# Encoder trunk on one core: the gate and up products of the large experts computed with the weights as the stationary operand

## What is computed

```
def swiglu(x, w_gate, w_up, w_down):
    return (jax.nn.silu(x @ w_gate) * (x @ w_up)) @ w_down

def moe_swiglu(x, w_router, w_gate, w_up, w_down):
    logits = (x @ w_router).astype(jnp.float32)
    top_v, top_i = lax.top_k(logits, TOP_K)
    gates = jax.nn.softmax(top_v, axis=-1)
    combine = jnp.sum(jax.nn.one_hot(top_i, N_EXPERTS, dtype=jnp.float32) * gates[..., None], axis=-2)
    out = jnp.zeros_like(x)
    for e in range(N_EXPERTS):
        out = out + combine[..., e:e + 1].astype(x.dtype) * swiglu(x, w_gate[e], w_up[e], w_down[e])
    return out
```

## Time and profile before

| | us |
|---|---|
| median of 3 runs | 1141.0 (1136.15 to 1141.62) |
| the profiled execution | 1139.2 |
| its span, from the first to the last instruction | 1137.3 |
| PE busy in the span | 1104.1 |
| PEld busy | 811.8 |
| DVE busy | 642.9 |
| ACT busy | 467.5 |

### The profile page before, as it was taken

One profiled execution on the slowest core, in us unless ns is written; L12 is line 12 of the kernel. 1 busy time (PEld: TensorE's weight loads), 2 busy tenths in 40 slices (PEclk: granted clock), 3 DMA queues, 4 the chain that ended last, 5 costly groups with the idle time before them and its releaser, 6 DMA issues.

```text
span 1137.3 us, 14580 instructions
## 1 busy us (share of the span) xinstructions
PE 1104.1 (97%) x5825; PEld 811.8 (71%) x5825; DVE 642.9 (57%) x745; ACT 467.5 (41%) x598; POOL 44.0 (4%) x45
## 2 busy tenths in 40 slices
PE   7999999999999999999999999999999999999996
PEld 6777878888877788776666666666666666666664
DVE  3887675445467886755655534554653465555235
ACT  4656444444335565143444423333343343443220
POOL 3000020000013000000000000000000000000001
PEclk9999999999999999989999999999999999999999
DMA  9943355555547600079999999899999989999972
GB/s 294 347 151 111 112 181 190 185 185 185 184 150 210 225 1 1 1 269 386 359 368 353 359 350 380 291 395 386 336 389 363 379 290 382 372 353 377 353 277 78
DMA packets 126815, 300.08 MB, mean 264 GB/s; under 512 B 4971, under 2 KB 7161, under 8 KB 126737
## 3 DMA queue, kind: packets, MB, share of 16 engines
q1 hardware_dynamic: 124336, 291.52, 71.1%
q0 software_dynamic: 2112, 6.87, 2.2%
q10 hardware_dynamic: 288, 0.63, 0.1%
HBM read 297.88 MB, written 1.12 MB: 263 GB/s over the span
## 4 chain that ended last, share of the span: by engine, by line
PE 88%; DMA 5%; DVE 2%; ACT 2%; issue 2%; POOL 0%; SPq 0%; POOLq 0%; DVEq 0%; ACTq 0%
PE bank L1595 23%; PE bank L1596 22%; PE bank L1657 12%; PE bank L2040 6%; PE bank L1685 6%; PE bank L2050 4%; PE bank L1768 3%; PE bank L1877 2%; DMA raw<-in_w_in 2%; PE bank L1862 1%; PE bank L1794 1%; PE bank L2018 1%; PE bank L1954 1%; DMA raw<-in_moe_w_gate 1%; PE bank L1600 1%
## 5 line engine op out<-in xcount | busy, mean ns | idle before, releaser
L1435 DVE TENSOR_TENSOR w_lo<-raw,w_hi 128x2048 fp32r<-128x2048 f32 x83 | 190.3, 2293 | 271.7 <-ACT w_hi L908 271.6
L1595 PE MATMUL bank<-w_hi,xT_hi 128*128 128x512 f32 (+1 forms) x832 | 331.7, 400 | 6.0 <-DVE xT_lo L1054 2.1
L1596 PE MATMUL bank<-w_hi,xT_lo 128*128 128x512 f32 (+1 forms) x832 | 321.7, 388 | 0.0
L908 ACT ACTIVATE w_hi<-raw 128x2048 fp32r<-128x2048 f32 x83 | 158.7, 1912 | 239.2 <-PE bank L1657 133.0
L1595 PEld LDWEIGHTS bank<-w_hi,xT_hi 128*128 128x128 f32 x832 | 157.1, 189 | 72.4 <-issue 28.5
L1031 DVE TENSOR_TENSOR w_lo<-raw,w_hi 128x2048 fp32r<-128x2048 f32 x62 | 141.9, 2291 | 104.8 <-ACT w_hi L727 104.4
L1596 PEld LDWEIGHTS bank<-w_hi,xT_lo 128*128 128x128 f32 x832 | 157.4, 189 | 28.8
L1657 PE MATMUL bank<-w_lo,xT_hi 128*128 128x512 f32 (+1 forms) x640 | 167.4, 384 | 0.0
L727 ACT ACTIVATE w_hi<-raw 128x2048 fp32r<-128x2048 f32 x64 | 122.6, 1918 | 99.5 <-PE bank L1657 45.9
L1657 PEld LDWEIGHTS bank<-w_lo,xT_hi 128*128 128x128 f32 x640 | 118.3, 188 | 24.2
L1595 PE MATMUL bank<-w_hi,hT_hi 128*128 128x512 f32 x312 | 124.7, 400 | 2.3 <-issue 2.3
(11 more groups left out here) (209 smaller groups left out, 1016.0 us busy)
## 6 DMA issues: line engine op xcount, KB each, us to landing
raw<-in_moe_w_up SPq DMA_DIRECT2D x70, 1024.0 KB, 8.8
raw<-in_moe_w_down SPq DMA_DIRECT2D x70, 1024.0 KB, 8.0
raw<-in_moe_w_gate SPq DMA_DIRECT2D x69, 1024.0 KB, 8.5
raw<-in_w_in SPq DMA_DIRECT2D x23, 1024.0 KB, 8.5
raw<-in_ffn_w_gate SPq DMA_DIRECT2D x11, 1024.0 KB, 5.1
raw<-in_ffn_w_up SPq DMA_DIRECT2D x11, 1024.0 KB, 5.1
raw<-in_ffn_w_down SPq DMA_DIRECT2D x11, 1024.0 KB, 5.0
raw<-in_w_out SPq DMA_DIRECT2D x8, 1024.0 KB, 5.9
```

Of the source, the lines that this page charges most:

```text
L908: nc.scalar.activation(w_hi[:, m % NH, :], raw[:, n % NR, :], ACT.Copy).then_inc(hi_done, 1)
L1435: nc.vector.tensor_tensor(w_lo[:, m % NH, :], raw[:, (BASE_MOE + load[at[o]]) % NR, :], w_hi[:, m % NH, :].bitcast(F32), ALU.subtract).the ...
L1595: nc.tensor.matmul(o, hi, wh, start=start, stop=False)
L1596: nc.tensor.matmul(o, lo, wh, start=False, stop=False)
```

## The change

`hidden_tiles` takes the place of `column_units` for the gate and up units of large experts. A 128 x 128 tile of the weights is stationary; one matmul moves the high and the low part of all 256 tokens past it side by side (512 columns; the new tile `xT` holds both parts next to each other), and one of 256 columns moves the high part past the low part of the weights. A unit is then 16 matmuls of 512 columns and 16 of 256. A chunk's gate or up result comes out as four tiles (`j`), hidden columns in the partitions, each in one bank: 256 columns of high and 256 of low part, which remain to be added. The tiles take five banks (0 to 4) in turn, `tile_bank`. DVE adds the two halves of each tile by a `tensor_reduce` (`read_tiles`) into `hidT`, the same memory as `hid`, or, for up, into a new tile `upT`; ACT applies silu to `hidT` in place and copies it to `hT_hi`; DVE multiplies and makes `hT_lo`. The transposes and their semaphore `e_psum` are gone; `tile_done` (PE to DVE) and `tile_read` (DVE to PE and ACT) are new.

```
-            def large_gate(c, eb):
-                if c > 0:
-                    act.wait_ge(e_psum, eb + 2 * c)
-                for tt in range(NT):
-                    ins = nc.scalar.activation(hid[:, tt, :], bank[:, tt, :], ACT.Silu)
-                ins.then_inc(silu_done, 1)
+            def large_gate(c, cb, tiles):
+                act.wait_ge(tile_read, tiles + (tile_at("gate", c, 3) + 1))
+                nc.scalar.activation(hidT, hidT, ACT.Silu).then_inc(silu_done, 1)
...
-            def large_up(c, cb, used):
-                dve.wait_ge(unit_used, used)
-                dve.wait_ge(silu_done, cb + (c + 1))
-                for tt in range(NT):
-                    ins = nc.vector.tensor_tensor(hid[:, tt, :], hid[:, tt, :], bank[:, NT + tt, :], ALU.mult)
-                ins.then_inc(hid_done, 1)
+            def read_tiles(kind, c, to, tiles, ends, used):
+                for j in range(4):
+                    if j < 3:
+                        dve.wait_ge(tile_done, ends + (3 * (2 * c + (kind == "up")) + j + 1))
+                    else:
+                        dve.wait_ge(unit_used, used)
+                    b = tile_bank(kind, c, j)
+                    nc.vector.tensor_reduce(to[:, j, :], bank[:, b, :].rearrange("p (h s) -> p s h", h=2),
+                                            AX.X, ALU.add).then_inc(tile_read, 1)
+            def large_gate(c, eb, tiles, ends, used):
+                if c > 0:
+                    dve.wait_ge(e_lo, eb + c)
+                read_tiles("gate", c, hidT, tiles, ends, used)
+            def large_up(c, cb, tiles, ends, used):
+                dve.wait_ge(hid_done, cb + c)
+                read_tiles("up", c, upT, tiles, ends, used)
+                dve.wait_ge(tile_read, tiles + (tile_at("up", c, 3) + 1))
+                dve.wait_ge(silu_done, cb + (c + 1))
+                nc.vector.tensor_tensor(hidT, hidT, upT[:], ALU.mult).then_inc(hid_done, 1)
...
+            def hidden_tiles(m, kind, c, part, tiles, off_l, halves=False):
...
+                    for j in range(4):
+                        if part == 0 and ks[0] == 0 and tile_at(kind, c, j) >= 5:
+                            pe.wait_ge(tile_read, tiles + (tile_at(kind, c, j) - 4))
+                        o = bank[:, tile_bank(kind, c, j), :]
+                        for k in ks:
+                            nc.tensor.matmul(o, wh[:, k, j * P:(j + 1) * P],
+                                             xT[:, 4 * part + k, :, :].rearrange("p h s -> p (h s)"),
+                                             start=part == 0 and k == 0, stop=False)
+                pe.wait_ge(lo_done, m + 1 + off_l)
+                for j in range(4):
+                    o = bank[:, tile_bank(kind, c, j), 0:SEQ]
+                    for k in range(4):
+                        ins = nc.tensor.matmul(o, wl[:, k, j * P:(j + 1) * P], xT_hi[:, 4 * part + k, :],
+                                               start=False, stop=part == 1 and k == 3)
...
-                    if who == "L" and kind == "gate":
-                        if part == 0:
-                            pe.wait_ge(silu_done, cb + c)
-                            if c == 0:
-                                pe.wait_ge(added, done + (added_at(units, "L", i - 1, 1) if i else 0))
-                        column_units(m, [part], 2, CW, xT_hi, xT_lo, range(NT), 0, off_l, halves=u == 0 and units is TRIO)
+                    if who == "L" and kind != "down":
+                        if (kind, c, part) == ("gate", 0, 0):
+                            pe.wait_ge(added, done + (added_at(units, "L", i - 1, 3) if i else 0))
+                        hidden_tiles(m, kind, c, part, tiles, off_l, halves=u == 0 and units is TRIO)
                     elif who == "L" and c < N_DOWN - 2:
                         if c == 0:
-                            pe.wait_ge(silu_done, cb + NCH)
-                            pe.wait_ge(hid_done, cb + NCH)
-                            pe.wait_ge(e_lo, eb + 2 * (NCH - 1))
+                            pe.wait_ge(tile_read, tiles + (N_TILES - 1))
+                            pe.wait_ge(e_lo, eb + (NCH - 1))
...
-                    if who == "L" and kind == "gate" and c > 0:
-                        large_transposes(c - 1, part, cb, eb)
-                    if who == "L" and kind == "down" and c < 2:
-                        large_transposes(NCH - 1, c, cb, eb)
```

More of the change, by code:

```diff
@@ L217, in encoder @@
         hid = row[:].rearrange("p (t n) -> p t n", t=NT)
+        hidT = row[:].rearrange("p (j s) -> p j s", s=SEQ)
         tab = sb("tab", [P, TABLE_W])
@@ L358, in encoder @@
         h_lo = sem("h_lo")
-        e_psum = sem("e_psum")
+        tile_done = sem("tile_done")
+        tile_read = sem("tile_read")
         e_hi = sem("e_hi")
@@ L411, in encoder, with tile_at, tile_bank @@
         SCATTER_BANKS = (6, 7, 5, 5)
+        N_TILES = 2 * NF
+        def tile_at(kind, c, j):
+            return (2 * c + (kind == "up")) * 4 + j
+        def tile_bank(kind, c, j):
+            return (tile_at(kind, c, j) + 4) % 5
         def gathers_behind(units):
@@ L975, in run_units @@
                     if who == "L":
-                        eb = fix((large + i) * (2 * NCH))
+                        cb, tiles = fix((large + i) * NCH + len(FFN_W)), fix((large + i) * N_TILES)
                     else:
@@ L981, in run_units @@
                     if (who, kind, part) == ("L", "gate", 1):
-                        act.wait_ge(unit_used, n + 1 + off)
-                        large_gate(c, eb)
+                        large_gate(c, cb, tiles)
                     if who == "S" and kind != "down" and part == 1:
@@ L991, in run_units @@
                         large_split(at, load, at.index(u) + AHEAD, off, use)
-                    if who == "L" and kind == "gate" and c > 0:
-                        large_hidden_hi(c - 1, part, eb)
-                    if who == "L" and kind == "down" and c < 2:
-                        large_hidden_hi(NCH - 1, c, eb)
+                    if (who, kind, part) == ("L", "gate", 0) and c > 0:
+                        large_hidden_hi(c - 1, cb)
+                    if (who, kind, c) == ("L", "down", 0):
+                        large_hidden_hi(NCH - 1, cb)
                     if who == "S" and (kind, part) == ("up", 0) and c > 0:
@@ L1524, in run_units @@
                     if who == "L":
-                        cb, eb = fix((large + i) * NCH + len(FFN_W)), fix((large + i) * (2 * NCH))
+                        cb, eb = fix((large + i) * NCH + len(FFN_W)), fix((large + i) * NCH)
+                        tiles, ends = fix((large + i) * N_TILES), fix((large + i) * (6 * NCH))
                     else:
@@ L1528, in run_units @@
                     add_outputs(u)
+                    if (who, kind, part) == ("L", "gate", 1):
+                        large_gate(c, eb, tiles, ends, used)
                     if (who, kind, part) == ("L", "up", 1):
-                        large_up(c, cb, used)
+                        large_up(c, cb, tiles, ends, used)
                     if (who, kind, part) == ("S", "gate", 1):
@@ L1536, in run_units @@
                         large_split(at, load, at.index(u) + AHEAD, off, off_l)
-                    if who == "L" and kind == "gate" and c > 0:
-                        large_hidden_lo(c - 1, part, eb)
-                    if who == "L" and kind == "down" and c < 2:
-                        large_hidden_lo(NCH - 1, c, eb)
+                    if (who, kind, part) == ("L", "gate", 0) and c > 0:
+                        large_hidden_lo(c - 1, eb)
+                    if (who, kind, c) == ("L", "down", 0):
+                        large_hidden_lo(NCH - 1, eb)
                     if (who, kind, c, part) == ("S", "up", 0, 1):
@@ L2010, in transpose_sel @@
                 ins.then_inc(selT_psum, 1)
-            def large_transposes(c, tt, cb, eb):
-                pe.wait_ge(hid_done, cb + (c + 1))
-                if c or tt:
-                    pe.wait_ge(e_lo, eb + (2 * c + tt))
-                for k in range(4):
-                    ins = nc.tensor.transpose(bank[:, 4, k * P:(k + 1) * P], hid[:, tt, k * P:(k + 1) * P], ident)
-                ins.then_inc(e_psum, 1)
+            def hidden_tiles(m, kind, c, part, tiles, off_l, halves=False):
+                slot = m % NH
+                wh = w_hi[:, slot, :].rearrange("p (k n) -> p k n", k=4)
+                wl = w_lo[:, slot, :].rearrange("p (k n) -> p k n", k=4)
+                if not halves:
+                    pe.wait_ge(hi_done, m + 1 + off_l)
+                for ks in ((0, 1), (2, 3)) if halves else ((0, 1, 2, 3),):
+                    if halves:
+                        pe.wait_ge(*((first_hi, 2) if ks[0] == 0 else (hi_done, m + 1 + off_l)))
+                    for j in range(4):
[12 more added lines that the diff above has]
+                                               start=False, stop=part == 1 and k == 3)
+                    if j == 3:
```

(3 more changed lines are left out.)

31 lines of the change are left out of this document (12 added, 19 removed).

## The result

| | before | changed |
|---|---|---|
| median, us | 1138.37 (1136.15 to 1141.81, 20 runs) | 1140.65 (1137.44 to 1143.24, 20 runs) |
| profiled execution's span, us | 1137.3 | 1138.2 |

The ratio is 1.0017, with a 95% interval of 1.0009 to 1.0025: the changed kernel is slower by 1.9 us (1.0 to 2.8; the two medians of the table are 2.3 us apart, and the text goes by the ratios). That is within the 0.5% that the prediction calls "same", and inside its range, but on the other side of the forecast sum of -2.2 us. That 1140.65 us lies less than 2 us above the forecast 1138.8 is luck: the forecast started from three runs with a median of 1141.0 us, 2.6 us above the median of the twenty, while the difference that it forecast is off by 4.1 us.

What follows compares the result with a forecast made beforehand. PE bounds, busy 97% of the span, with the loop of split, load and use just under it. Terms -12.3 + 5.8 + 4 - 0.9 + 1.2 = -2.2 us: 1139 us against the median 1141.0, range 1132 to 1154.

Steps and rivals of the forecast that it cites:

- parts 1 and 2: PE in the large experts' gate and up units: transposes gone, -12.3 us; matmuls in another shape, +5.8 us.
- Part 3: DVE's reductions and ACT's work per chunk: DVE rises to 70%, PE never waits for the reads of banks, 0 us.
- PE waits for banks: Rival: small units' sums make DVE late to the tiles, half a microsecond at each of 28 turns, 1153 us; chance 0.07.
- The third rival: DVE's reductions over pairs 1 KB apart cost twice the price, 1.37 us each, giving 1169 us; chance 0.10.
- Part 4: Low parts behind gate and up part 1 end later, 23.8 us in all, freeing slots of `raw` late: +4 us.
- PE that goes faster eats the same leads: Argument against the rival that PE gets its whole gain (-6.2 us, 1134.8 us; chance 0.20).
- Part 5: Two down products wait less, -0.9 us; second large expert's first gate unit waits for all four additions, +1.2 us.
- The slot loop: Rival: SP's wait for low parts behind gate and up part 1 becomes the bound, up to +17.6 us, 1158.6; chance 0.16.

Runs made afterwards that it cites:

- one transpose of four: The kernel before with one of each four transposes of a large expert made and three left out, 9.2 us less PE work; ratio 0.9932 to the kernel before.

## Why the prediction was wrong

**Bound and PE's pace (parts 1 and 2): right.** Take all of PE's waits for loads and for DVE out of the expert stage (from its first large matmul to its last), and 629.4 and 629.6 us remain in the two profiles of the kernel before, 622.4 and 622.5 in those of the changed one: -7.0 us. That counts as gone the two waits ahead of the down products (0.5 us each, "issue" in the rows of the kernel before); at the second a wait of 0.4 us for a read took its place, so PE's path is 6.6 us shorter. The terms said -12.3 + 5.8 - 0.9 = -7.4.

The Trainium skill's rule that weight load and matmul together set the spacing, so that its formula for one matmul alone comes out too low for short ones ("TensorE: Matmul & The Clock Gate", section "Back-to-back issue gap"), agrees in its direction: 256 columns started 0.120 us apart, not 0.109. That the weight load is the cause no run here shows, and for 512 columns, where the same section gives 131 ns in such a stream, the measured 0.227 us decides.

**Part 3, DVE: durations right, the zero wrong by 0.8 us.** Reads of 0.68 us, DVE at 66% where 70% was said. But the ring of banks is not free. At two places a part-0 unit follows an up part 1 with nothing between, and at one of them DVE was still with the small expert's sums when the tiles were ready; DVE and PE in order of time:

```profile
644.29 0.68 DVE L1469 TENSOR_TENSOR hid_s<-hid_s,up_s 32x512 f32<-32x512 f32 x1
644.90 1.27 DVE L1479 TENSOR_REDUCE upT<-bank 128x256 f32<-128x512 f32 x2
```

```profile
643.91 1.09 PE L2053 MATMUL bank<-xT,w_hi 128*128 128x512 f32 x4
645.63 1.66 PE L2053 MATMUL bank<-xT,w_hi 128*128 128x512 f32 x6 [0.62 <-DVE upT L1479]
```

That is the rival "PE waits for banks", with its mechanism and at its place, once and not 28 times. The third rival, slow reads, fell with the 0.68 us, and with it what the Trainium skill ("Advanced Engine Details and Errata", section "PSUM Cachelines") would give if carried from matmuls to DVE.

**Part 4, late low parts: the step that failed, by its size.** The lateness was 14 x (1.18 + 0.73) = 26.7 us (25.5 in the second profile) against 23.8 forecast: up part 1 as forecast, gate part 1 late by 1.18 us and not 1.0. Its price at the old pace was right, 15% measured and 14% forecast, and 26.7 x 0.15 = 4.0 us is the +4 of the sum. What the sum lacked is a term for the pace itself. "PE that goes faster eats the same leads" stood under a rival as an argument and nowhere as microseconds, although a share of the gain's own size was at stake; alone it costs 1.9 us of 9.2 (one transpose of four), so some 1.3 of 6.5. Worked out from the experiments the whole term is 4.0 + 1.3 = 5.3 us; behind 530 us the changed kernel waited 5.3 to 5.6 us longer for loads than the kernel before, and 4 was said.

**Part 5.** The second expert's first gate unit waits as forecast (PE and DVE answer to the earlier trace rows): 1.2 us.

```profile
810.06 1.92 PE L2086 MATMUL bank<-raw,xs 128*32 128x512 f32 x16
813.12 2.11 PE L2053 MATMUL bank<-xT,w_hi 128*128 128x512 f32 x8 [1.14 <-DVE acc L1499]
```

```profile
811.67 1.40 DVE L1499 SCALAR_TENSOR_TENSOR acc<-bank,comb,acc 128x512 f32<-128x512 f32 x2
```

Of the 0.9 us at the two down products only one half came; at the other PE waited for a read instead, the last row of the first list of waits.

**The sum with what was measured:** -6.6 + 5.5 (loads) + 0.8 (bank) + 1.2 (additions) = +0.9 us, where the forecast had -2.2. The ratio gives +1.9 (1.0 to 2.8). The remaining 1.0 us I can't place: it is less than the first loads of the stage differ from one execution to the next.

**The slot loop as a rival** was the right mechanism: it decides the sign, though it passed on a fifth (5.5 of 26.7 us, the pace's share included) and not the half from which it was to count as slower. A gain of 6.6 us stands against losses of 7.5, and errors of 0.4 to 1.5 us in four terms were enough to turn the sign.

## What to carry to other kernels

When PE is made faster in a kernel whose loads are close behind it, charge the gain itself: here a fifth came back as waits for loads with no other change. What frees the slot of a load belongs ahead of work that nobody waits for: the same changed kernel went from 1.0017 to 0.9938 of the time before when the split of the weights was put ahead of silu and of the product, at no cost to the instructions. And where a change lengthens an engine's work between two duties, write down for each of its instructions who waits for it, and order them by that before judging the change.

## What the runs showed of the hardware

A reduction by DVE over pairs of PSUM values 1 KB apart costs what a contiguous one costs (0.68 us for 512 values a partition). A matmul's beat did not depend on which operand was stationary: 0.227 us for 512 columns and 0.120 us for 256 on either side. And 370 GB/s into one core was sustained through a 193 us stretch, where the changed kernel's 362 looked like a limit by its busy share of 0.98; the busy share of the DMA didn't tell a full queue from a late one.
